# Filter constants loaded ahead, the context dots spread over the whole projection, and one comparison for two one-hot tables

## What is computed

```
# implicit filters of the long convolution, for X and for C
h = sin(freq * (feat @ hy_w1 + hy_b1))          # feat: L x 33, a constant
h = sin(freq * (h @ hy_w2 + hy_b2))             # 64 wide
h = (h @ hy_w3 + hy_b3).reshape(L, 2, 2, 512) * window     # window: a constant
filt_fft = rfft(taps made of h and normed)      # with a constant DFT table
...
p = u @ w_in                                    # q, k | v | g | GLU pairs | long convolution | gates
...
# product-key expert layer, per token
s = einsum(q, sub_keys); s_top, i_top = top_k(s, 16)       # 8 heads x 2 halves x 128 keys
best_s, best_j = top_k(all pair sums, 16); gates = softmax(best_s)
experts = i_top[first half] * 128 + i_top[second half]     # 128 picks of 16384 per token
a = einsum(u_tab[experts], h)                   # the "dots"
out = einsum(gelu(a) * gates, v_tab[experts])   # the "adds"
```

## Time and profile before

| | us |
|---|---|
| median of 3 runs | 6211.31 |
| the profiled execution's own time | 6212.44 |
| its span, first to last instruction | 6210.5 |
| PE busy | 5078.8 (82%) |
| DVE busy | 4306.7 (69%) |
| ACT busy | 1872.9 (30%) |
| POOL busy | 860.5 (14%) |

### The profile page before, as it was taken

The page is one execution under the profiler, slowest core; times in us unless marked ns, Lnnn a source line. Parts: engine busy times, 40 slices in busy tenths (PEclk is TensorE's granted clock), DMA queues, the critical chain, the costliest instruction groups (busy, mean ns, idle before and its releaser), DMA issues. The chain is left out here.

```text
span 6210.5 us, 70543 instructions
## 1 busy us (share of the span) xinstructions
PE 5078.8 (82%) x23958; PEld 4052.2 (65%) x23958; DVE 4306.7 (69%) x7529; ACT 1872.9 (30%) x3261; POOL 860.5 (14%) x644
## 2 busy tenths in 40 slices
PE   7697737779667677999999968979794659999998
PEld 5285626633456465998888737723573559999997
DVE  1547577748786597999999952358635977767676
ACT  0123312122112265333333311221122653333333
POOL 0000005500243000333333300000000001111110
PEclk8797868989789787999999979979897779999999
DMA  6142217711465255999999912201121347777775
GB/s 212 65 156 68 98 48 274 289 41 41 161 236 200 75 159 173 387 396 397 395 394 384 362 66 78 89 20 58 52 88 41 82 139 272 274 273 275 275 272 193
DMA packets 465786, 1173.18 MB, mean 189 GB/s; under 512 B 225468, under 2 KB 259677, under 8 KB 412575
## 3 DMA queue, kind: packets, MB, share of 16 engines
q1 hardware_dynamic: 373474, 634.44, 30.3%
q0 software_dynamic: 92160, 536.91, 22.6%
HBM read 1107.01 MB, written 64.23 MB: 189 GB/s over the span
## 5 line engine op out<-in xcount | busy, mean ns | idle before, releaser
L2145 POOL DMA_INDIRECT arena<-in_peer_uv,kept x384 | 518.9, 1351 | 3675.3 <-POOLq L2030 2038.4
L223 PE MATMUL psum<-h_hi,u_ring_hi 128*128 128x384 f32 x2048 | 694.5, 339 | 13.1 <-DVE ring_lo L2233 13.0
L223 PE MATMUL psum<-h_hi,ring_lo 128*128 128x384 f32 x2048 | 694.9, 339 | 0.0
L223 PE MATMUL psum<-h_lo,u_ring_hi 128*128 128x384 f32 x2048 | 694.0, 339 | 0.0
L223 PE MATMUL psum<-v_ring_hi,w_hi 128*128 128x512 f32 x1536 | 609.7, 397 | 6.2 <-DVE ring_lo L2238 6.2
L223 PE MATMUL psum<-ring_lo,w_hi 128*128 128x512 f32 x1536 | 604.1, 393 | 0.0
L223 PE MATMUL psum<-v_ring_hi,w_lo 128*128 128x512 f32 x1536 | 600.6, 391 | 0.0
L2238 DVE TENSOR_TENSOR ring_lo<-kept,v_ring_hi 128x1024 fp32r<-128x1024 f32 x256 | 313.8, 1226 | 300.3 <-ACT v_ring_hi L2193 295.2
L2277 DVE SCALAR_TENSOR_TENSOR arena<-arena 128x1024 f32<-128x1024 f32 x384 | 482.1, 1283 | 19.5 <-issue 0.4
L2265 DVE CUSTOM_DVE_ANT_0 arena<-arena 128x1024 f32<-128x1024 f32 x384 | 463.1, 1220 | 30.6 <-DMA arena<-in_peer_uv,kept 29.9
L2205 ACT ACTIVATE w_hi<-arena 128x384 fp32r<-128x384 f32 x256 | 134.7, 526 | 965.7 <-DVE arena L2248 965.7
(11 more groups left out here) (349 smaller groups left out, 10334.3 us busy)
## 6 DMA issues: line engine op xcount, KB each, us to landing
kept<-in_mix SPq DMA_DIRECT2D x312, 512.0 KB
kept<-in_peer_u SPq DMA_DIRECT2D x256, 512.0 KB
kept<-in_peer_uv SPq DMA_DIRECT2D x256, 512.0 KB
kept<-in_ada SPq DMA_DIRECT2D x96, 512.0 KB
gate_scratch<-arena SPq DMA_DIRECT2D x12, 4096.0 KB, 21.0
arena<-gate_scratch SPq DMA_DIRECT2D x128, 384.0 KB, 6.1
spec_scratch<-arena SPq DMA_DIRECT2D x4, 2048.0 KB, 8.5
arena<-in_k_dft_x SPq DMA_DIRECT2D x6, 1024.0 KB, 11.9
```

The costliest lines, as they stand in the source:

```text
L223: done = pe.matmul(out, lhs[x], rhs[y], start=first and j == 0, stop=last and j == 2)
L2145: pool.indirect_dma_start(rows[q % NBUF], None, peer_uv, bass.IndirectOffsetOnAxis(ap=row_id[q % G][:, q // G:q // G + 1], axis=0))\
```

## The change

Three parts.

1. The loads of the filter stages are moved. In the first block SP now also loads, behind the five inputs, the three filter weights of layer 0, the features of C and X, and the window and DFT table of C (8, 16, 520, 33, 66, 1024 and 256 KB, 1.97 MB). The filter stage of X in layer 0 loads only its window and table at its start. In `stage_merge_experts` of layer 0 SP loads all six for the filter stage of layer 1. Weights and features have new places that no earlier stage uses at that time.
2. The dots of the projection are spread anew: 24 with q and k, 40 with v, 24 with g, 26 with GLU (3, 3, 3, 4, 3, 3, 3, 4), 14 with hp (1, 1, 1, 1, 1, 2, 1, 1, 1, 1, 1, 2). The last 14 use two other buffers, in the place of ACT's sigmoid results; POOL gathers into these once all GLU blocks are evacuated. The hp loop is unrolled on DVE.
3. The two comparisons of a chunk become one of twice the size. ACT and PE now wait for that one.

```diff
+        def load_filter_weights(sp, l):
+            at = M0 + 33920
+            sp.dma_start(area(at, HID)[0:EMB, :], hw1[l]).then_inc(filter_in[0].sem, 16)
+            sp.dma_start(area(at + 64, HID)[0:HID, :], hw2[l]).then_inc(filter_in[0].sem, 16)
+            sp.dma_start(area(at + 128, 2048)[0:HID + 1, :], hw3[l]).then_inc(filter_in[0].sem, 16)
+        def load_filter_features(sp, s):
...
+            sp.dma_start(area(M0 + 36096 + (512 if s == "C" else 0), T)[0:EMB, :], k_feat).then_inc(filter_in[0].sem, 16)
+        def load_filter_tables(sp, s):
...
+            sp.dma_start(area(M0 + 4224, nt * 1024), k_win).then_inc(filter_in[1].sem, 16)
+            sp.dma_start(area(M0 + 16512, nt * T_OF[s]), k_dft[0]).then_inc(filter_in[2].sem, 16)
                 sp.dma_start(fin_g, final_g).then_inc(consts_in.sem, 16)
+                load_filter_weights(sp, 0)
+                load_filter_features(sp, "C")
+                load_filter_features(sp, "X")
+                load_filter_tables(sp, "C")
                 sp.wait_ge(consts_in.sem, consts_in.at(80))
...
-                    sp.dma_start(feat[0:EMB, :], k_feat).then_inc(consts_in.sem, 16)
-                    sp.dma_start(w1[0:EMB, :], hw1[l]).then_inc(consts_in.sem, 16)
-                    sp.dma_start(w2[0:HID, :], hw2[l]).then_inc(consts_in.sem, 16)
-                    sp.dma_start(w3[0:HID + 1, :], hw3[l]).then_inc(consts_in.sem, 16)
-                    sp.dma_start(win.rearrange("p a b c -> p (a b c)"), k_win).then_inc(gates_in[0].sem, 16)
-                    sp.dma_start(dft.rearrange("p a b c -> p (a b c)"), k_dft[0]).then_inc(gates_in[1].sem, 16)
+                    if l == 0 and s == "X":
+                        load_filter_tables(sp, s)
...
-                    pe.wait_ge(consts_in.sem, consts_in.at(64))
+                    pe.wait_ge(filter_in[0].sem, filter_in[0].at(ready))
...
+            late = [area(m["ret"] + 1024 * k, D) for k in range(2)]
+            LATE = 14
+            EARLY = P - LATE
+            dots_of = shares(24, 8) + shares(40, 8, 24) + shares(24, 8, 64) + shares(EARLY - 88, 8, 88) + shares(LATE, 12, EARLY)
...
-                        gather_ctx(pool, peer_rows, bufs, 0, P)
+                        gather_ctx(pool, peer_rows, bufs, 0, EARLY)
+                        pool.wait_ge(bank_free.sem, bank_free.at(32 + 4))
+                        gather_ctx(pool, peer_rows, late, EARLY, P, EARLY)
...
-                        skewed(dve, 8, rest(8), with_dots(keep_g, 64, 4), False, True, beside)
-                        skewed(dve, 8, rest(16), with_dots(keep_glu, 96, 4), True, True, beside)
+                        skewed(dve, 8, rest(8), with_dots(keep_g, 16), False, True, beside)
+                        skewed(dve, 8, rest(16), with_dots(keep_glu, 24), True, True, beside)
...
-                        skewed(dve, 12, rest(24), keep_hp, True, False)
+                        skewed(dve, 12, rest(24), with_dots(keep_hp, 32), True, False, beside)
...
-                        pe.wait_ge(dve_b.sem, dve_b.at(CHUNKS * t + n + 1))
+                        pe.wait_ge(equal_ready.sem, equal_ready.at(CHUNKS * t + n + 1))
...
-                            dve.tensor_tensor(hot_i[n % 3], iota4, at_i[:, at].unsqueeze(2).broadcast_to([P, 4, NK]),
+                            dve.tensor_tensor(hot[n % 3], iota4, picked_t[:, 0:2, at].unsqueeze(3).broadcast_to([P, 2, 4, NK]),
                                               ALU.is_equal).then_inc(equal_ready.sem, 1)
-                            dve.tensor_tensor(hot_j[n % 3], iota4, at_j[:, at].unsqueeze(2).broadcast_to([P, 4, NK]),
-                                              ALU.is_equal).then_inc(dve_b.sem, 1)
...
+                if l < DEPTH - 1:
+                    @block.sync
+                    def _(sp):
+                        load_filter_weights(sp, l + 1)
+                        load_filter_features(sp, "X")
+                        load_filter_tables(sp, "X")
```

More of the change, by code:

```diff
@@ L286, in build, with gather_ctx @@
         ctx_out = area(8192, D)
-        def gather_ctx(pool, table, bufs, first, end):
+        def gather_ctx(pool, table, bufs, first, end, freed=0):
             for q in range(end - first):
                 if q >= len(bufs):
-                    pool.wait_ge(ctx_free.sem, ctx_free.at(q - len(bufs) + 1))
+                    pool.wait_ge(ctx_free.sem, ctx_free.at(freed + q - len(bufs) + 1))
                 pool.indirect_dma_start(bufs[q % len(bufs)], None, table,
@@ L295, in gather_ctx, with ctx_dots @@
                     .then_inc(ctx_rows_in[q % len(bufs)].sem, 16)
-        def ctx_dots(dve, bufs, first, end):
+        def ctx_dots(dve, bufs, first, end, start=0, turns=0):
             for q in range(first, end):
-                k = q % len(bufs)
-                dve.wait_ge(ctx_rows_in[k].sem, ctx_rows_in[k].at(16 * (q // len(bufs) + 1)))
+                n = q - start
+                k = n % len(bufs)
+                dve.wait_ge(ctx_rows_in[k].sem, ctx_rows_in[k].at(16 * (turns + n // len(bufs) + 1)))
                 dve.tensor_tensor_reduce(bufs[k], bufs[k], ctx_h, 1.0, 0.0, ALU.mult, ALU.add, ctx_weight[:, q:q + 1])\
@@ L632, in _ @@
                                 j += 1
-            consts_in.add(64)
-            for c in gates_in:
+            if not (l == 0 and s == "C"):
+                filter_in[0].add(ready)
+            for c in filter_in[1:]:
                 c.add(16)
@@ L811, in _, with with_dots @@
                     hstep = T + 2
-                    def with_dots(keep, first, each):
+                    def with_dots(keep, first):
                         def finish(i, k):
                             keep(i, k)
-                            at = first + each * (4 * i + k)
-                            ctx_dots(dve, bufs, at, at + each)
+                            at, end = dots_of[first + 4 * i + k]
+                            if first < 32:
+                                ctx_dots(dve, bufs, at, end)
+                            else:
+                                ctx_dots(dve, late, at, end, EARLY, EARLY // len(bufs))
                         return finish if beside else keep
@@ L827, in _ @@
                         dve.wait_ge(ctx_in.sem, ctx_in.at(32))
-                    skewed(dve, n_qk, rest(0), with_dots(keep_qk, 0, 3), False, False, beside)
+                    skewed(dve, n_qk, rest(0), with_dots(keep_qk, 0), False, False, beside)
                     if beside:
                         for n in range(8):
-                            with_dots(keep_v, 24, 5)(n // 4, n % 4)
+                            with_dots(keep_v, 8)(n // 4, n % 4)
                     else:
@@ L852, in stage_project @@
                 ctx_in.add(32)
-                counted_ctx(bufs, P)
+                counted_ctx(bufs, EARLY)
+                counted_ctx(late, LATE)
             act_a.add(KC)
@@ L1676, in stage_select @@
             picked_t = area(small, 3, 128)
-            at_i, at_j, weight = (picked_t[:, n, :] for n in range(3))
+            weight = picked_t[:, 2, :]
             a = M0 + 6144
@@ L1686, in stage_select @@
             match = area(a + 2048, 8, TOPK, TOPK)
-            hot_i, hot_j = ([area(at + 512 * n, 4, NK) for at in (M0 + 4096, M0 + 5120, a + 5120)] for n in range(2))
+            hot = [area(at, 2, 4, NK) for at in (M0 + 4096, M0 + 5120, a + 5120)]
+            hot_i, hot_j = ([x[:, n] for x in hot] for n in range(2))
             q3 = qp[:, 0:8 * T].rearrange("p (h t) -> p h t", t=T)
             iota16 = iota[:, 0:TOPK].unsqueeze(1).unsqueeze(1).broadcast_to([P, 8, TOPK, TOPK])
-            iota4 = iota.unsqueeze(1).broadcast_to([P, 4, NK])
+            iota4 = iota.unsqueeze(1).unsqueeze(1).broadcast_to([P, 2, 4, NK])
             def tile_of(n):
```

19 lines of the change are left out of this document (12 added, 7 removed).

## The result

The changed kernel takes 6158.14 us, the median of 5 runs (6145.07 to 6168.38), against 6214.29 for the kernel before on the same chip (5 runs, 6208.68 to 6236.13): ratio 0.9903, 95% interval 0.9887 to 0.9919. A second set of runs gave 6161.89 and 0.9904 (0.9890 to 0.9919). The forecast of 6160 and its range (6147 to 6180) held.

What follows compares the result with a forecast made beforehand. Each stage has its own bound: load waits at filter starts, PE and DVE's residual in the projection, DVE in selection. -20.2 - 21.9 - 9 = -51.1 from 6212.4 gives 6161.3, as median 6160; range 6147 to 6180 us.

Steps and rivals of the forecast that it cites:

- Part 1: Three filter stages: waits for loads at the stage's start vanish; -20.2 us, between -21 and -14.
- Part 2: Projection from g's first block on: respread dots cut PE's waits for DVE's residual; -21.9 us, bounds -30 and -12.
- g: Projection, g with three dots: DVE ends at 6.0 against PE's 5.6; 1.5 us lost in 8 blocks.
- GLU: Projection, GLU: two odd blocks with 4 dots 1.5 us late each, the other two 0.37; 3.7 us lost.
- Supply: Projection, g and GLU: POOL's gathers barely keep pace with the dots; 2 us of new waits, bounds 0 and 8.
- hp: Projection, hp: with two buffers, the second dot of a two-dot block waits 2 to 3 us; 1.5 us lost.
- The end: End of the projection: two dots behind the last evacuation, the second waiting for its buffer; 4.7 us added.
- Part 3: Selection of both layers: one comparison saves 0.05 us in each of 192 chunks; -9 us, between +2 and -13.
- The longer loop decides: Selection: DVE waits for PE in every chunk, 0.55 us 192 times, +106; total 6267 us; chance 0.03.
- The supply: Projection: row supply bounds g and GLU, or hp's two buffers do; gain only 12, total 6170 us; chance 0.22.
- The start: First block: early loads hold the inputs or weight stream by their 4.8 us; total 6165 us; chance 0.12.
- The doubled comparison no cheaper: Selection: no gain from one comparison, or waits for ada weights absorb it; 0 to +2, total 6170 us; chance 0.10.

Runs made afterwards that it cites:

- part 3 alone: The kernel before with only the two comparisons of a chunk made one of 1024: 6208.46 us, ratio 0.9990 (0.9979 to 1.0002).
- single parts: The kernel before with only the filter loads moved (6193.36 us), only the dots spread anew (6195.64) or only the single comparison (6208.46).

## Why the prediction was right

**Part 1: -20.2, right.** From the load of the parameters (C, layer 1) or of C's spectrum store (X) to the first product: C 14.95 before, 7.65 after; layer 1 14.47 and 7.69; X 13.92 and 6.80. That is -7.3, -6.8, -7.1 = -21.2, and +0.6 at the start where I had put 0.4. From the first product of the experts' merging to the load of the next parameters are 10.7 us (3520.83 to 3531.53) with 3.7 MB loaded beside it, and were 10.4 (3570.73 to 3581.15): the cover was real. Unforeseen: in 7 of the 10 executions with part 1, X's transform is another 2.2 to 2.8 us shorter, because the clock comes back earlier. PE starts the filter stage at 0.50 of full speed; it was back at full speed 33.0 us behind the first product before (229.1) and 30.1 after (211.3); the windows behind it show 0.89 against 0.99:

```profile
226.00:240.00 14.00, 14.00 (x30) 5.95 (x29) 7.42 (x12) 4.71 (x8) 0.00 (x0) 0.89 0.00 1
```

```profile
211.00:225.00 14.00, 14.00 (x33) 6.14 (x33) 8.76 (x14) 4.70 (x8) 0.00 (x0) 0.99 0.00 1
```

In those seven the clock is back 29.7 to 30.4 us behind the first product; in the other three, and in the three traces without part 1, 32.1 to 33.0. Why is not shown, and it is not a gain to count on.

**Part 2: -21.9, right** with -23.2 in the three traces of the table that have it, in part by luck: two misses nearly cancel. The stretch of 27 blocks became 161.5 us, 10.3 above PE's pace, where I had 8.7. *g*: 0.6 us in the first evacuation and 5.94 a block instead of 5.8; a short wait costs PE 0.63 us and not 0.37, since the first product behind it comes 0.86 us after the one before (1099.27 to 1100.13) instead of 0.23. *GLU*: 49.1 us for eight blocks, 4.3 above pace (forecast 3.7). *Supply*: 1.5 us in three waits (forecast 2, bound 8). In g and GLU a gather took 1.49 us and 0.30 to the next, against 92 / 44 = 2.1 us for each dot, so the margin was 0.3 us and not the wide one that POOL's waiting suggests. The Trainium skill's rule that I had weighed ("SBUF — State Buffer", "Who interferes with whom") would have made the gain 18. The gather is slower than beside an idle DVE, as by that rule, but it was no slower than before: 1.49 us with DVE busy 84% of g and GLU before, 1.49 with 85% after. The 92% that I had assumed did not come. *hp*: 3.0 instead of 1.5, and not for buffers, for which DVE waited 0.6 us once: PE waited 1.9 us for the residual behind GLU's last block of four dots, and then the clock fell for 3.4 us (0.86 on average from 1178 to 1190), so that the second block took 7.64 us. *The end*: +1.8 and not +4.7. The second dot had its row already, and the next stage waits for its own table anyway, which hides the rest.

**Part 3: -9, right in size by a wrong balance, and so partly by luck.** The two selections give -8.4 and -7.3 in the two profiles and -7.1 with part 3 alone. I took 0.05 us a chunk; it is 0.07, 6.6 us of DVE time in layer 1 (302.58 to 295.95 in the earlier trace rows's stretch and in 323 us after). The row that I read stood for the 26 chunks with the longer distance, 1.37, and not for the 159 at 1.2; the difference is nearly the same in both. The +1.1 at the last chunk did not come: the store of the gates is issued 17.3 to 17.7 us before DVE's last instruction, before and after, and in layer 0 DVE waits 3.7 us for its landing either way. In its place the later signal costs 0.6 us in layer 1, a term that I did not have: I looked at the loop over the buffers and not at what stands behind ACT's last chunk of a tile, PE's next scores. -6.6 + 0.6 = -6.0 is what layer 1 gave (-5.9 and -6.0). And layer 0 keeps only part: PE stands still for ada blocks there, which cost DVE 8.4 us ahead of a comparison, and DVE waits for the turned picks, where it then arrives sooner, 13.7 us instead of 9.8.

**Rivals.** *The longer loop decides*: DVE waited for PE in layer 0 three times instead of once, 9.2 us against 8.6; the loop never closed. *The supply*: 1.5 us. *The start*: 0.6. *The doubled comparison no cheaper*: its instruction is; of all four this came nearest, since part 3 alone is not told from nothing by its interval; the selection of layer 1 does tell it, -5.9 to -6.0 against 0.0 and -0.7 without part 3. That medians of single parts sum to 46 and the whole to 54 to 56 stays unexplained within its uncertainty.

## What to carry to other kernels

A load at the head of a stage is free to move if the stage before leaves the DMA idle, but not ahead of a point where all engines meet: three microseconds of issuing there delayed everything by 2 (one run). When side work is spread over a stage, look for the block that overfills its engine and not for the mean: a wait of 2 us in a dense matmul stream cost its own length here and, when the clock fell behind it, as much again. Before a signal is moved, list every duty of the engine that receives it, also the one behind the loop; and before a longer wait is called its price, look whether the work inside the wait ran at the same clock. And where a gain stays away in one of two like stages, compare the waits of the two: here that led to 18 us more in the selection of layer 0, more than either layer had gained from the change.

## What the runs showed of the hardware that I had not expected

- A load issued 4 us behind a 4 MB store on the same queue held SP for 16.63 us; behind two stores of 2 MB the loads held it for 6.24 and 10.46. So a store can hold up a load that is issued behind it, and with it everything behind SP, and halving the store doesn't shorten the sum.
- The same 16 products of the scores took 4.05 to 6.29 us in layer 1, as the granted clock had it, and moved DVE's waits by more than the signal that was under test.
- A PE that has waited 0.47 us restarts 0.63 us late: the next product starts 0.86 us after the last instead of 0.23.
- The same filter stage, with the same products at the same distances, got the full clock back 30 us behind its first product in seven executions and 32 to 33 in six.
- One operation of 1024 elements is 1.12 us to the next instruction, two of 512 are 1.19: halving the count saves 0.07 us, a tenth of the shorter one's 0.68.
